# A mixture-of-experts loop on one core: who casts the expert inputs, and in which place of the queues

## The reference

```python
xb = xpad[tok_b]
h = jax.nn.silu(xb @ w_gate[e]) * (xb @ w_up[e])
return h @ w_down[e]
```

## Time and profile before

| | us |
|---|---|
| median of 3 runs | 1744.66 (1743.45 to 1745.66) |
| the profiled execution | 1749.66, span 1747.6 |
| PE busy | 1628.3 (93%) |
| DVE busy | 1249.0 (71%) |
| ACT busy | 780.7 (45%) |
| POOL busy | 393.5 (23%) |

### The profile page before, as it was taken

The page is one execution under the profiler, slowest core; times in us unless marked ns, Lnnn a source line. Parts: engine busy times, 40 slices in busy tenths (PEclk is TensorE's granted clock), DMA queues, the critical chain, the costliest instruction groups (busy, mean ns, idle before and its releaser), DMA issues.

```text
span 1747.6 us, 24578 instructions
## 1 busy us (share of the span) xinstructions
PE 1628.3 (93%) x9324; PEld 1305.9 (75%) x9324; DVE 1249.0 (71%) x1537; ACT 780.7 (45%) x1021; POOL 393.5 (23%) x184
## 2 busy tenths in 40 slices
PE   7995899999999997999988999999999999999997
PEld 7855555555555554988678999999999978888886
DVE  5244888878888886765315996566777788888886
ACT  4413777767777774456033334666666400000000
POOL 6601211111111110000234889422222100000000
PEclk9996899999999998999999999999999999999999
DMA  8407799999999988533312444444444555555553
GB/s 315 154 1 302 304 421 409 415 373 392 421 408 411 413 345 275 193 121 121 145 49 92 175 169 166 150 148 151 141 152 150 187 193 186 194 194 194 192 192 120
DMA packets 45902, 398.87 MB, mean 228 GB/s; under 512 B 10120, under 2 KB 12424, under 8 KB 13576
## 3 DMA queue, kind: packets, MB, share of 16 engines
q1 hardware_dynamic: 45832, 397.89, 59.4%
HBM read 395.77 MB, written 3.01 MB: 228 GB/s over the span
## 4 chain that ended last, share of the span: by engine, by line
PE 38%; POOL 6%; issue 4%; DMA 1%; DVE 1%; ACT 0%; DVEq 0%; POOLq 0%; SPq 0%
PE bank L1834 19%; PE bank L1771 9%; POOL rest L1010 6%; PE bank L1775 5%; PE bank L1805 3%; PE bank L763 1%; DMA raw<-in_v 1%; POOL ring_rest L742 0%; DVE lead L2305 0%; DVE h L2404 0%; ACT half_lead L736 0%; DVE hid_lo L2379 0%; DVE h L2407 0%; DVE xhat L656 0%; DVEq L188 0%
## 5 line engine op out<-in xcount | busy, mean ns | idle before, releaser
L2067 DVE TENSOR_TENSOR ring_rest<-ring,w_lead 128x2048 fp32r<-128x2048 f32 x128 | 293.4, 2343 | 37.7 <-ACT w_lead L1144 37.7
L1144 ACT ACTIVATE w_lead<-ring 128x2048 fp32r<-128x2048 f32 x128 | 239.4, 1905 | 22.1 <-DVE ring_rest L2067 21.7
L647 ACT ACTIVATE xhat<-h 128x1024 f32<-128x1024 f32 x6 | 6.3, 1057 | 432.9 <-DVE h L2404 351.8
L1571 PE MATMUL bank<-ring_rest,x_two 128*128 128x512 f32 x512 | 140.9, 408 | 31.7 <-DVE ring_rest L2067 31.7
L1289 ACT ACTIVATE lead<-raw 128x2048 fp32r<-128x2048 f32 x64 | 122.4, 1913 | 88.7 <-PE bank L1775 88.7
L1834 PE MATMUL bank<-lead,hid_hi 128*128 128x512 f32 x512 | 157.9, 390 | 2.7 <-DVE hid_lo L2379 2.6
L1834 PE MATMUL bank<-lead,hid_lo 128*128 128x512 f32 x512 | 157.7, 389 | 0.0
L1834 PE MATMUL bank<-rest,hid_hi 128*128 128x512 f32 x512 | 157.6, 389 | 0.0
L1571 PE MATMUL bank<-w_lead,x_two 128*128 128x512 f32 x512 | 145.9, 423 | 11.8 <-POOL x_two L993 6.6
L1775 PE MATMUL bank<-nT_hi,rest 128*128 128x256 f32 x1024 | 144.7, 284 | 9.7 <-POOL rest L1010 9.7
L742 POOL TENSOR_TENSOR ring_rest<-ring,half_lead 128x2048 fp32r<-128x2048 f32 x20 | 92.4, 4627 | 264.2 <-ACT half_lead L736 255.0
(11 more groups left out here) (331 smaller groups left out, 2831.0 us busy)
## 6 DMA issues: line engine op xcount, KB each, us to landing
ring<-in_w_gate SPq DMA_DIRECT2D x32, 2048.0 KB, 9.4
ring<-in_w_up SPq DMA_DIRECT2D x32, 2048.0 KB, 9.6
ring<-in_w_down SPq DMA_DIRECT2D x32, 2048.0 KB, 10.4
raw<-in_u SPq DMA_DIRECT2D x64, 1024.0 KB, 4.8
raw<-in_v SPq DMA_DIRECT2D x64, 1024.0 KB, 4.8
ring<-in_w_in SPq DMA_DIRECT2D x14, 2048.0 KB, 10.1
ring<-in_w_out SPq DMA_DIRECT2D x4, 2048.0 KB, 7.8
ring<-in_w_q SPq DMA_DIRECT2D x4, 2048.0 KB, 7.9
```

Of the source, the lines that this page charges most:

```text
L1144: act.activation(w_lead[half][:, :, :], ring8(slot)[:, 4 * half:4 * half + 4, :], ACT.Copy).then_inc(w_lead_ready, 1)
L1571: last = pe.matmul(bank[kind][:, :], x_two[j][:, 4 * half + k, :], part[:, k, :], start=(ready is w_lead_ready and half == 0 and k == 0), ...
L2067: dve.tensor_tensor(ring_rest8(slot)[:, part, :], ring8(slot)[:, part, :], w_lead[half][:, :, :].bitcast(F32), ALU.subtract).then_inc(w_re ...
```

## The change

GpSimd leaves the branch altogether. ScalarE now casts straight from `xs` at the dynamic address (it loads the register itself) and does so for expert e+1, behind `turned(e-1)` and a wait for PE to be done with expert e-1, ahead of `low` of e. VectorE makes the rest of e+1 straight from `xs`, between the gate rests and the up rests of e, behind a wait for ScalarE's cast of e+1. `share_of` moves from behind even experts to between the gate rests and this subtraction in odd experts. Expert 0's inputs are made ahead of the loop. The buffers `x_two` stay two.

```diff
-            with pool.Else():
-                def expert_input(e, j, peeled):
-                    first = pool.value_load(starts_i[0:1, bass.ds(e, 1)], min_val=0, max_val=SLOTS)
...
             with act.Else():
+                def high_input(e, j):
+
+                    first = act.value_load(starts_i[0:1, bass.ds(e, 1)], min_val=0, max_val=SLOTS)
+                    act.activation(x_two[j][:, :, 0:BLOCK], xs[:, :, bass.ds(first, BLOCK)], ACT.Copy).then_inc(x_hi_ready, 1)
+
...
-                    act.wait_ge(x_ready, e + 1)
-                    act.activation(x_two[j][:, :, 0:BLOCK], x_blk[j][:, :, :], ACT.Copy).then_inc(x_hi_ready, 1)
+                        act.wait_ge(xs_act, KD // 2)
+                        act.wait_ge(xs_dve, KD // 2)
+                        act.wait_ge(xs_zero, 1)
+                        high_input(e, j)
                     split_lead(e, pair, j, 0, first, [1] if first else range(2))
                     if not peeled:
                         copy_out(e - 2, j, bank[3])
                     split_lead(e, pair, j, 1, False)
                     if j or not peeled:
                         turned(e - 1, 1 - j)
+                    if not last:
+                        if not first:
+                            act.wait_ge(w_used, 2 * e)
+                        high_input(e + 1, 1 - j)
                     low(e, j, 0)
                     silu(e, j)
                     low(e, j, 1)
...
-                def expert_vector(e, j):
-                    split_rest(e, j, 0)
-                    split_rest(e, j, 1)
...
+                def low_input(e, j):
+
+                    first = dve.value_load(starts_i[0:1, bass.ds(e, 1)], min_val=0, max_val=SLOTS)
+                    dve.wait_ge(x_hi_ready, e + 1)
+                    dve.tensor_tensor(x_two[j][:, :, BLOCK:], xs[:, :, bass.ds(first, BLOCK)], x_two[j][:, :, 0:BLOCK].bitcast(F32),
+                                      ALU.subtract).then_inc(x_lo_ready, 1)
...
+                def expert_vector(e, j, shared=None, last=False):
+                    split_rest(e, j, 0)
+                    if shared is not None:
+                        share_of(*shared)
+                    if not last:
+                        low_input(e + 1, 1 - j)
+                    split_rest(e, j, 1)
+                    total(e, j, 0)
+                    total(e, j, 1)
```

More of the change, by code:

```diff
@@ L1167, in copy_out, with expert_scalar @@
                     last.then_inc(y_act, 1)
-                def expert_scalar(e, pair, j, peeled):
+                def expert_scalar(e, pair, j, peeled, last=False):
                     first = peeled and j == 0
@@ L1187, in _ @@
                     expert_scalar(j, 0, j, True)
-                with act.Fori(1, PAIRS) as pair:
+                with act.Fori(1, PAIRS - 1) as pair:
                     for j in range(2):
                         expert_scalar(2 * pair + j, pair, j, False)
+                for j in range(2):
+                    expert_scalar(N_EXPERTS - 2 + j, PAIRS - 1, j, False, j == 1)
                 turned(N_EXPERTS - 1, 1)
@@ L2093, in share_of @@
                     dve.tensor_tensor(share[:, 0, :], share[:, 0, :], share[:, 1, :], ALU.add).then_inc(share_ready, 1)
-                dve.wait_ge(rows_kept, 2)
[L2096 to L2106, removed]
+                def expert_vector(e, j, shared=None, last=False):
[7 more added lines that the diff above has]
+                    total(e, j, 1)
+                    dve.wait_ge(up_sum, e + 1)
+                    dve.wait_ge(sil_ready, e + 1)
+                    dve.tensor_tensor(hid[j][:, :], hid[j][:, :], upv[j][:, :], ALU.mult).then_inc(hid_ready, 1)
+                dve.wait_ge(rows_kept, 2)
+                dve.wait_ge(xs_act, KD // 2)
+                dve.wait_ge(xs_dve, KD // 2)
+                dve.wait_ge(xs_zero, 1)
+                low_input(0, 0)
+                expert_vector(0, 0)
+                expert_vector(1, 1)
+                expert_vector(2, 0)
+                expert_vector(3, 1, (0, True))
+                with dve.Fori(2, PAIRS - 1) as pair:
+                    expert_vector(2 * pair, 0)
+                    expert_vector(2 * pair + 1, 1, (pair - 1, False))
+                expert_vector(N_EXPERTS - 2, 0)
+                expert_vector(N_EXPERTS - 1, 1, (PAIRS - 2, False), True)
                 share_of(PAIRS - 1, False)
```

## The result

The changed kernel takes 1875.5 us (1874.0 to 1876.1) against 1745.2 us of the kernel before in the same session: 1.0745 of its time, 95% interval 1.0728 to 1.0762. The profiled span grew from 1747.6 to 1872.3 us. The forecast was 1878 us.

What follows compares the result with a forecast made beforehand. PE and VectorE were taken to share the bound on the expert loop. The median 1744.66 us plus 88 for the new wait, net of gains and start, plus 45 for the clock gave 1878 us, range 1820 to 1922.

Steps and rivals of the forecast that it cites:

- rival C: Whole kernel faster, the cast being there before VectorE asks; DMA floor 29.3 us a pair; 1725 us, chance 0.04.
- (1): GpSimd's two instructions leave; `mult` on VectorE falls from 1.67 to 0.68 us; with the cast's move, 2.0 us a pair gained.
- (2): ScalarE's cast, 0.5 us, leaves the place ahead of the gate's leads; with GpSimd's leaving, 2.0 us a pair gained.
- rival D: `mult` on VectorE keeps its 1.67 us, contention not being GpSimd's: +9 us inside A or Rival B; no separate chance given.
- (3): VectorE's subtraction waits for ScalarE's cast with up rests queued behind: turn to product end 8.8 us, before 4.4 and 5.0.
- A cast that starts 0.4 us behind the copy: Sign of being wrong on ScalarE: the register load hidden altogether, where 0.95 us from copy to cast was taken.
- (4): Share matrix on VectorE moves into the new wait, which covers its 1.1 us; without that wait, 1.1 us a pair.
- (5): DMA engines in the expert loop fall from full to about 343 GB/s; nothing waits for them.
- The start: Ahead of the first product: first lead 172.3, cast 173.0, subtraction 173.7, so 2.2 us earlier than 175.94.
- The clock: PE's clock falls to 1.2 GHz in 22 of 31 experts, about 2.05 us each, 45 us; bounds 0 and 96.
- Rival B: Same new wait before VectorE's subtraction, but PE's clock holds: 1833 us, 1816 to 1850; chance 0.26.
- A: New wait before VectorE's subtraction plus PE's clock falling in many experts: about 1850 to 1922 us, taken at 1878; chance 0.66.

Runs made afterwards that it cites:

- 1718 us kernel: The kernel after with VectorE's order changed to gate rests, up rests, share, total gate, subtraction of e+1, total up, `mult`: 1718.3 us, 0.9844 of before.

## Why the prediction was right, point by point

**What bounded the loop.** PE and VectorE by turns, with DMA not far below: the kernels with another order on VectorE reach 1732 and 1718 us, and at the second DMA takes over, at the 29.3 us a pair that rival C named as its floor. C's 1725 us was too high: it left out the two falls of the loop before, 6 us, which the 1718 us kernel hasn't.

**(1), (2), the 2.0 us a pair.** The hop from the down behind an even product to the next turn was forecast at 8.2 us and is 8.2 us in the kernel with PE kept busy (400.09 to 408.29 in its trace). `mult` fell to 0.68 us. The contention is GpSimd's, so rival D is out; but it belongs to GpSimd's work and not to `mult`, as the kernel with the wait behind `mult` shows.

**(3), the new wait.** The mechanism stands: cut at either of two places, the chain loses its whole cost. Of the 8.8 us from the turn to the end of the product there are 8.5 at full clock (427.67 to 436.15 in the kernel with PE kept busy). The term that was mis-sized is the register load on ScalarE. I took 0.95 us from the copy's start to the cast's; it is 0.34 (646.35 to 646.69). The 0.95 was no measured gap either: in the earlier trace rows the instruction ahead takes 1.28 us and the load ends beside it. "A cast that starts 0.4 us behind the copy" was one of my own signs of being wrong, and it came true; by the prediction a hidden load is worth 31 x 0.55 = 17 us at most. ScalarE's load in that stretch, in the kernel after (ns min/median/max, first and last start):

```profile
L1119 ACTq TENSOR_LOAD <-starts_i x1: 277/277/277, 646.1 to 646.1; - x1
L1119 ACTq SEQ_ASSERT  x1: 18/18/18, 646.6 to 646.6; - x1
```

It starts at 646.1, ahead of the copy's start at 646.35, while ScalarE works at the last up lead (642.61 + 3.71 = 646.3). PE's turn was over and the copy stood ready behind that lead, so the load ran beside both. The kernel with the share back has the opposite case: there the turn (352.45) ends just ahead of the lead (351.36 + 1.91 = 353.3), the load starts at 353.3 as the copy does, and the cast comes 0.58 us behind the copy. The lead also makes the copy start 1.10 us behind the turn in the kernel after, not 0.85. From turn to cast it is 1.44 us and not 1.80. With about 0.32 us too much in each of 31 experts (8.8 for 8.48 in even ones, for 8.4 in odd ones, 408.29 to 416.68) I was 10 us too high: 88 - 10 = 78, and the kernel with PE kept busy is 80 us above before.

**(4) the share.** In the wait it costs nothing, as forecast. That it would be worth 1.1 us a pair on VectorE's path in the other order was too much: with the share back it is 0.65 us a pair on PE, and the time moves by 2 us within overlapping intervals.

**(5) DMA.** Forecast 343 GB/s; it is 321 with the falls and 349 without them.

**The start.** Forecast 2.2 us earlier; it is 3.5 (175.94 to 172.43). Of these 2.2 lie between ScalarE's first lead (170.41 before, 169.07 after) and the first product, as forecast; the other 1.3 lie ahead of the loop and aren't explained here.

**The steps.** Forecast 17.0 and 19.7 us without the clock. ScalarE's casts in the kernel with PE kept busy:

```profile
590.10 0.64 ACT L1120 ACTIVATE x_two<-xs 128x512 fp32r x1
609.49 0.64 ACT L1120 ACTIVATE x_two<-xs 128x512 fp32r x1
626.18 0.64 ACT L1120 ACTIVATE x_two<-xs 128x512 fp32r x1
```

and in the kernel after:

```profile
587.02 0.63 ACT L1120 ACTIVATE x_two<-xs 128x512 fp32r x1
608.40 0.63 ACT L1120 ACTIVATE x_two<-xs 128x512 fp32r x1
625.97 0.64 ACT L1120 ACTIVATE x_two<-xs 128x512 fp32r x1
646.69 0.64 ACT L1120 ACTIVATE x_two<-xs 128x512 fp32r x1
665.54 0.63 ACT L1120 ACTIVATE x_two<-xs 128x512 fp32r x1
```

Without the falls the steps are 19.4 and 16.7 us, 72.2 for four. With them four take 78.5: 1.6 us a fall.

**The clock.** Rival B, the same wait at full clock, would have been 1833 (1824.9 as measured with PE kept busy); it was A. The 45 us came from 22 falls at 2.05 us. Measured are 51 us, and both factors were off: a fall in every expert, 30 in the loop, rather than in 7 of 10, and 1.6 us each rather than 2.05. By the steps 30 x 1.6 = 48 us. The one fall that I priced at 3.1 us was 6.8 us long; of the four shown here two are as long and two last little over 3 us. That part of each is hidden beside VectorE's chain is my reading and not shown. So the 1878 us for 1875.5 rest on two errors of opposite sign, 88 for 80 us of wait and 45 for 51 of clock, and the second on two more. That the sum came within 3 us is luck. What was right is the mechanism, both of its parts, and the bounds.

The Trainium skill ("TensorE: Matmul & The Clock Gate", HAM oscillation) puts the fall down to one long idle gap. Here the longest wait of PE for rests is 2.6 us, the waits come in pairs (2.49 and 1.01 us, with four matmuls between them), and the clock fell in every expert. Its next section ("A second HAM failure mode: psum-queue depth-cycling") describes another kernel, but the same pattern, a clock that falls and rises where PE is idle for short times between groups of matmuls. That fits, and filling the idle times took the falls away.

## What to carry to other kernels

Before a step is moved "one ahead", follow its new wait backwards, and look at what is queued behind it. Here the wait ends only with PE's turn, which stands behind VectorE's own last gate rest, and the up rests that PE needs next are queued behind the wait. So the engine idles for the whole chain, and PE after it, however little the step costs. Give the waiting instruction a place where what it needs is there by the time the engine comes to it; here the same instructions in another order take 1718 us instead of 1875. And when PE gets idle stretches, price the clock too: it was 51 of 130 us, and PE's busy share, 90% of the span, doesn't show it.

## What the runs showed of the hardware that was not expected

Extra matmuls that compute nothing of use made the kernel 51 us faster (1875.5 to 1824.9) by keeping the granted clock at 1.00 instead of 0.87. A register load for a dynamic address leaves VectorE idle for 0.49 us behind a 0.42 us instruction, 0.52 behind a 0.68 us one, and for no time behind a 2.28 us one. On ScalarE it is hidden even behind a 0.38 us copy if that copy itself stands ready in the queue behind a longer instruction, and costs 0.20 us where the copy becomes ready only as that one ends. GpSimd's two instructions lengthened each VectorE instruction seen beside them, 0.68 to 1.67 us or 0.43 to 1.39, so that shifting them by one instruction moved the loss and did not change the time. With more loads waiting in the queue (21.4 us to land, not 14.7) DMA stayed at 428 GB/s over 100 us.
